# Output projections and MLP starts of a two-layer kernel: weight panels rounded one step earlier in the program, and the sum of squares behind the first MLP panel

## The reference

```
x = x + (o * silu(r)) @ w_out                       # output projection, 1024 x 1024
x = x + square(relu(rms_norm(x, g) @ w1)) @ w2      # MLP, 1024 -> 4096 -> 1024
```

## Time and profile before

| | us |
|---|---|
| median of three runs | 1702.68 |
| the profiled execution, its own time | 1700.87 |
| its span, first to last instruction | 1698.8 |
| TensorE busy | 1627.7 (96%) |
| VectorE busy | 975.7 (57%) |
| ScalarE busy | 686.7 (40%) |
| GpSimd busy | 242.0 (14%) |

### The profile page before, as it was taken

How to read it: one execution, slowest core, us unless ns; L and a number is a source line. 1 busy time by engine, 2 the same in 40 slices (tenths; PEclk the granted TensorE clock), 3 DMA queues, 4 the chain that set the end, 5 groups by cost and what they waited for, 6 DMA issues and landing times.

```text
span 1698.8 us, 24770 instructions
## 1 busy us (share of the span) xinstructions
PE 1627.7 (96%) x9418; PEld 1304.7 (77%) x9418; DVE 975.7 (57%) x1500; ACT 686.7 (40%) x1040; POOL 242.0 (14%) x222
## 2 busy tenths in 40 slices
PE   6999978999999999999799999999999999999998
PEld 3777757888888887667457888878787788888887
DVE  5555645444444457787466768586774544444443
ACT  6455543323232355424455445362543432323232
POOL 0234330000000033143200403104040000000000
PEclk7999989999999999999899999999999999999999
DMA  4222213333333334223103122131220333333333
GB/s 132 74 72 65 63 38 87 87 99 99 99 92 101 92 98 119 63 66 86 37 4 108 40 75 75 51 87 51 65 62 26 88 104 93 99 95 102 87 100 99
DMA packets 258158, 135.07 MB, mean 80 GB/s; under 512 B 10699, under 2 KB 254940, under 8 KB 258068
## 3 DMA queue, kind: packets, MB, share of 16 engines
q1 hardware_dynamic: 258068, 133.84, 28.1%
HBM read 131.64 MB, written 2.18 MB: 79 GB/s over the span
## 4 chain that ended last, share of the span: by engine, by line
PE 78%; DVE 9%; issue 7%; ACT 4%; POOL 1%; DMA 0%; DVEq 0%; POOLq 0%; PEldq 0%; ACTq 0%; SPq 0%; PEld 0%
PE bank L231 18%; PE bank L233 18%; PE bank L232 18%; PE bank L1680 4%; PE bank L493 3%; PE bank L495 3%; PE bank L494 3%; DVE arena L1985 2%; DVE w_lo L215 2%; ACT w_hi L211 1%; PE bank L1260 1%; PE bank L1514 1%; PE bank L1696 1%; PE bank L1733 1%; DVE arena L2127 1%
## 5 line engine op out<-in xcount | busy, mean ns | idle before, releaser
L211 ACT CAST w_hi<-raw 128x1024 fp32r<-128x1024 f32 x234 | 245.0, 1047 | 260.4 <-PE bank L233 237.3
L231 PE MATMUL bank<-m_hi,w_hi 128*128 128x512 f32 x856 | 337.5, 394 | 6.0 <-POOL w_lo L221 2.8
L233 PE MATMUL bank<-m_hi,w_lo 128*128 128x512 f32 x856 | 334.3, 391 | 0.0
L232 PE MATMUL bank<-m_lo,w_hi 128*128 128x512 f32 x856 | 334.3, 391 | 0.0
L215 DVE TENSOR_TENSOR w_lo<-raw,w_hi 128x1024 fp32r<-128x1024 f32 x218 | 271.2, 1244 | 102.4 <-ACT w_hi L211 100.6
L231 PE MATMUL bank<-h_hi,w_hi 128*128 128x512 f32 x640 | 256.2, 400 | 10.6 <-DVE w_lo L215 6.2
L232 PE MATMUL bank<-h_lo,w_hi 128*128 128x512 f32 x640 | 252.7, 395 | 0.0
L233 PE MATMUL bank<-h_hi,w_lo 128*128 128x512 f32 x640 | 252.4, 394 | 0.0
L231 PEld LDWEIGHTS bank<-m_hi,w_hi 128*128 128x128 f32 x856 | 161.5, 189 | 43.1 <-issue 5.5
L232 PEld LDWEIGHTS bank<-m_lo,w_hi 128*128 128x128 f32 x856 | 161.5, 189 | 34.4 <-issue 1.2
L233 PEld LDWEIGHTS bank<-m_hi,w_lo 128*128 128x128 f32 x856 | 161.4, 189 | 33.9
(11 more groups left out here) (282 smaller groups left out, 2264.4 us busy)
## 6 DMA issues: line engine op xcount, KB each, us to landing
raw<-in_l_w_ff SPq DMA_DIRECT2D x64, 512.0 KB, 4.0
raw<-in_w_in SPq DMA_DIRECT2D x64, 512.0 KB, 3.8
raw<-in_w_mlp_up SPq DMA_DIRECT2D x32, 512.0 KB, 4.0
raw<-in_w_mlp_down SPq DMA_DIRECT2D x32, 512.0 KB, 4.0
raw<-in_l_w_in SPq DMA_DIRECT2D x24, 512.0 KB, 3.8
raw<-in_l_w_out SPq DMA_DIRECT2D x8, 512.0 KB, 3.7
arena<-gb_rows SPq DMA_DIRECT2D x16, 256.0 KB, 4.7
raw<-in_w_out SPq DMA_DIRECT2D x8, 512.0 KB, 4.1
```

What stands on the lines that cost most here:

```text
L211: act.copy(w_hi[q.par][:], raw[q.par][:]).then_inc(s["w_hi_ready"], 1)
L231: pe.matmul(g_bank[q.par][:], w_hi[q.par][:, k], hi[:, k], start=(k == 0), stop=False)
L232: pe.matmul(g_bank[q.par][:], w_hi[q.par][:, k], lo[:, k], start=False, stop=False)
L233: last = pe.matmul(g_bank[q.par][:], w_lo[q.par][:, k], hi[:, k], start=False, stop=(k == KT - 1))
```

## The change

Four things are moved, and no arithmetic is added or removed.

- In `act_wout` and `dve_wout` the split of panel k + 2 stands in round k, where the split of panel k + 1 stood: on ScalarE ahead of the high half and the square, on VectorE right behind the add of panel k and ahead of its low half and accumulation. The splits are the same in number and order.
- The ones matmul is taken out of `pe_wout` (now `pe_mlp_sum`) and stands behind the first of the MLP's panels. Ln and Exp (now `act_mlp_root`) stand in the MLP's second step on ScalarE, behind the split that this step begins with.
- So that the first group of each MLP can hold these, it is written out on TensorE and ScalarE; the loop has two rounds instead of three there. On VectorE the loop keeps its three rounds.
- The 39 clears are spread over the rounds k = 2 to 5 of the first projection, and the increments of `hid_ready` and `down_done` follow the projection.

```diff
@@ -839,19 +839,22 @@
             with pe.Fori(0, KT // 2 - 1) as m:
                 for u in range(2):
                     pe_panel(pe, Panel(base + 2, 2, m, u), *lay_mid[i])
+
+        def pe_mlp_sum(pe, i):
             pe.wait_ge(s["w_acc"], KT * (i + 1))
             pe.matmul(b[0][:], ones[:], mlp_acc, start=True, stop=True).then_inc(s["w_ss"], 1)
 
         def act_wout(act, base, i, gain):
             for k in range(KT):
                 q = Panel(base, 0, 0, k)
-                if k:
-                    act_split(act, q.next())
+                if k < KT - 1:
+                    act_split(act, q.next().next())
                 act.wait_ge(bank_free[q.par], q.k + 2)
                 act.activation(lay_in[i][0][:, k], x[:, k], ACT.Copy, scale=gains[:, gain + k:gain + k + 1]).then_inc(s["w_hi"], 1)
                 if k >= 2:
                     act.wait_ge(s["w_acc"], KT * i + k - 1)
                 act.activation(mlp_sq[:, k % 2], x[:, k], ACT.Square).then_inc(s["w_sq"], 1)
+        def act_mlp_root(act, i):
             act.wait_ge(s["w_ss"], i + 1)
             act.activation(r_sqr, b[0][:], ACT.Ln, scale=1.0 / D, bias=eps[:]).then_inc(s["w_ln"], 1)
             act.wait_ge(s["w_ln"], i + 1)
@@ -860,10 +863,10 @@
         def dve_wout(dve, base, i, gain):
             for k in range(KT):
                 q = Panel(base, 0, 0, k)
-                if k:
-                    dve_split(dve, q.next())
                 wait_panel(dve, q)
                 dve.tensor_tensor(x[:, k], x[:, k], g_bank[q.par][:], ALU.add).then_inc(bank_free[q.par], 1)
+                if k < KT - 1:
+                    dve_split(dve, q.next().next())
                 dve.wait_ge(s["w_hi"], KT * i + k + 1)
                 dve.scalar_tensor_tensor(lay_in[i][1][:, k], x[:, k], gains[:, gain + k:gain + k + 1],
                                          lay_in[i][0][:, k].bitcast(F32), ALU.mult, ALU.subtract).then_inc(s["h_ready"], 1)
@@ -873,6 +876,9 @@
                 else:
                     dve.wait_ge(s["w_acc"], KT * i + k)
                     dve.tensor_tensor(mlp_acc, mlp_acc, mlp_sq[:, k % 2], ALU.add).then_inc(s["w_acc"], 1)
+                if i == 0 and 2 <= k <= 5:
+                    for done in (gla_sems + gate_sems)[k - 2::4]:
+                        dve.sem_clear(done)
 
         sems("rl sqr hid_hi hid_ready down_done dn x_fin f_sq f_acc f_ss f_ln f_r f_t f_x f_h f_hi y_ps y_sb")
 
@@ -886,27 +892,32 @@
 
         def pe_mlp(pe, base, i, first):
 
-            def group(g, last_mlp):
+            def group(g, last_mlp, first_group=False):
                 for u in range(8):
                     pe_panel(pe, Panel(base, 16, g, u), *lay_in[i], s["h_ready"] if u == 0 else None, first)
+                    if first_group and u == 0:
+                        pe_mlp_sum(pe, i)
                 for u in range(8):
                     pe_panel(pe, Panel(base, 16, g, 8 + u), *lay_mid[i], s["hid_ready"] if u == 0 else None,
                              KT * GROUPS * i + KT * g + 2)
                     if last_mlp and u >= 1:
                         pe_out(pe, u - 1)
 
-            with pe.Fori(0, GROUPS - 1) as g:
+            group(0, False, True)
+            with pe.Fori(1, GROUPS - 1) as g:
                 group(g, False)
             group(GROUPS - 1, i == 1)
 
         def act_mlp(act, base, i):
             n = KT * GROUPS * i
 
-            def group(g, last):
+            def group(g, last, first_group=False):
                 for u in range(16):
                     q = Panel(base, 16, g, u)
                     if not (last and i == 1 and u == 15):
                         act_split(act, q.next())
+                    if first_group and u == 1:
+                        act_mlp_root(act, i)
                     if u < 8:
                         wait_panel(act, q)
                         act.wait_ge(s["hid_ready"], n + KT * g + u + 1)
@@ -920,7 +931,8 @@
                     elif last and u >= 9:
                         act_out(act, u - 9)
 
-            with act.Fori(0, GROUPS - 1) as g:
+            group(0, False, True)
+            with act.Fori(1, GROUPS - 1) as g:
                 group(g, False)
             group(GROUPS - 1, True)
             if i == 0:
@@ -2279,11 +2291,9 @@
             dve_gates(dve)
             dve_gla(dve)
             fence(dve, 2)
-            for done in gla_sems + gate_sems:
-                dve.sem_clear(done)
+            dve_wout(dve, N_WO0, 0, G_FFN0)
             dve.sem_inc(s["hid_ready"], 2)
             dve.sem_inc(s["down_done"], 1)
-            dve_wout(dve, N_WO0, 0, G_FFN0)
             dve_mlp(dve, N_FF0, 0)
             dve.sem_inc(s["att_done"], 1)
             dve_in1(dve)
```

## The result

| | before | after |
|---|---|---|
| median of the five runs of the first comparison, us | 1700.27 | 1685.59 |
| lowest to highest, us | 1695.72 to 1703.55 | 1681.68 to 1686.08 |
| the profiled execution, own time, us | 1700.87 | 1685.93 |
| its span, us | 1698.8 | 1684.1 |

The ratio of the times is 0.9908, with a 95% interval of 0.9887 to 0.9929. In two later comparisons the same kernel had 0.9895 (0.9875 to 0.9916) and 0.9900 (0.9880 to 0.9921). Between the medians the difference was 14.7 us in the first comparison, 17.3 and 18.5 in the two later ones. The forecast was 1685, within 1678 to 1693.

A forecast was written before the change was run, and what follows sets the result against it. TensorE, busy 96% of the span, was taken as the bound, so only its holes and slow stretches could be won. Gains of 4.0 + 4.9 + 7.8 = 16.7 us took 1700.87 to 1684.2, called 1685, range 1678 to 1693.

The forecast's parts named there:

- The sum: Gains at four places, 16.7 us off 1700.87: 1684.2, called 1685 because the runs' median was 1.8 above the profiled execution.
- A: Third panel of the first projection: loses 4.2 us to hole and low clock; 4.0 gained, 0.2 us hole left.
- B: Start of the first MLP: 4.7 us lost, 3.0 hole and 1.7 low clock; all of it gained.
- D: Start of the second MLP: 3.1 us lost to a 2.92 us hole, no slow matmul behind; all gained.
- C: Third panel of the second projection: 6.2 us lost; 4.9 gained, a 1.3 us hole left without low clock.
- the sign named for A: First matmul of panel 2 within 0.3 us of the end of panel 1, no slow matmul after it.
- The clears: 39 semaphore clears before the first projection's add: VectorE is free for A only because they go; spreading them costs nothing.
- The second MLP panel: Panel after the moved ones matmul: subtraction done by 294.9 us, wanted at 296.9, so not late.
- rival 1: Low clock comes anyway, so only holes are won: 10.4 us, 1690.5; chance 0.13.
- rival 2: Only the MLP starts gain, another wait holding the panels' rounding: 7.8 us, 1693; chance 0.09 together with rival 4.
- rival 4: No change as measured: parts of rival 1 and rival 2, 6 to 8 us gain, 1693 to 1695; 0.09 with rival 2.
- rival 3: Slower: the MLPs' written-out group waits for its code; at 1 us per panel 1716 us; chance 0.03.

The follow-up runs named there:

- e1: Kernel after with only the splits two panels ahead and the spread clears, ones matmul and loops as before; 1689.58 us, 0.9931 of the kernel before.
- e4: Kernel after with the 39 clears put back in front of the first projection; 1681.28 us, 0.9885 of the kernel before.
- e2: Kernel after with only the sum of squares behind the first MLP panel, splits and clears as before; 1691.33 us, 0.9943 of the kernel before.
- e3: Kernel before with each MLP's first group written out on TensorE and ScalarE, nothing moved; 1699.32 us, 0.9989 of the kernel before.
- e5: Kernel before with 6 to 13 unused matmuls in each of its four holes, nothing moved; 1694.93 us, 0.9972 of the kernel before.
- run 16: Not a label of a run: a verb and a count, in "engines that run 16 more panels of straight code"; no measured time belongs to it.
- e7: e6 with 12 unused matmuls on TensorE just ahead of the first fence; 1680.76 us, 0.9892 of the kernel before.
- e8: The kernel of e7 measured again; 1677.97 us, 0.9873 of the kernel before.
- e6: Kernel after with each projection's third panel running its 16 high-half matmuls before the 8 low-half ones; 1680.29 us, 0.9890 of the kernel before.

## Why the prediction was right

**The sum.** 16.7 us were forecast; 16.5 are measured in the stages, 14.7 in the median of the first comparison, and 18.6 between the medians over all runs (1700.8 of 50 runs, 1682.2 of 17). The mechanism is shown: in the traces the waits at A, B and D shrink or go, that at C shrinks to the size forecast, and the gain lies in the two stages. That the 1685 met the median of 1685.59 so closely is luck. It is 0.8 us above the sum, where the reason given for it was a difference of 1.8, and the 17 runs of the kernel after spread from 1679.2 to 1686.2.

**A.** 4.0 forecast, 3.8 measured by e1. The chain from the end of panel 0 over cast and subtraction came to 0.1 us where I put it. The hole of 0.2 us is not fixed: where the low clock ends earlier, panel 1 ends earlier too, and the hole is 0.75 us (252.66 to 253.64 less one turn, in the second profile). The stage is as long either way (60.90 to 61.05). But the sign named for A, a first matmul within 0.3 us of the end of panel 1, thus held in the first profile of the kernel after alone, and there the first matmul behind it was still slow.

**The clears.** The step "VectorE is free for it only because the 39 semaphore clears go from there" was wrong in its size. It named what held VectorE, and the clears did fill the time until the add. But after the reordering the add alone no longer sets when the subtraction starts; the cast ends level with it, and it hid them (e4).

**B and D.** 4.7 and 3.1 forecast. B is 4.7 in e2. D cannot be read alone from e2, whose stage 2 holds a change at C too. The ones matmul costs 0.86 us, not 0.94, which leaves the gain almost as it is, since both kernels have it. The second MLP panel was no new wait.

**C.** 4.9 forecast. The hole that stays was forecast as 1.3 and is 1.34. That it would bring no low clock held in all four profiles that have it (three of the kernel after, and e4). In e1 it held too, and the low clock came behind D. The 6.2 us that C was said to lose, 3.0 of it low clock, were those of one trace. Read in the same way, C lost 5.0 us in e2 and 4.8 in e3, which leaves 3.5 to 3.6 to be won, and D lost 4.7 instead of 3.1 in e3. C and D together are sound (9.3 us before, 9.5 in e3, 7.9 of it won); the split between them is one trace's chance.

**The rivals.** That the low clock comes anyway (rival 1) fell twice: in the traces of after, and in e5, where the holes alone were changed. Its doubt was sound in another form, though: a hole and the slow stretch behind it do not go together one to one (C and D in e1, e2 and e3), and runs differ by their clock even in the untouched stretches. At an equal mean clock of 0.986 the kernel before has 1695.4 us (2 runs) and the kernel after 1683.8 (5 runs), 11.6 us apart, which is about what the holes alone are (10.4). The rest of the 18.6 is a higher clock, some 6 us of it the slow matmuls behind the holes. That only the MLP starts gain (rival 2) fell with e1, and with it rival 4. The written-out group (rival 3) fell with e3; its text names VectorE among the engines that run 16 more panels of straight code, but VectorE kept its three rounds, and e3 wrote the group out on TensorE and ScalarE as the change does.

**Page and trace.** At the MLP's loop edges no wait is to be seen: TensorE is busy 340.00 of 340 us, and with one branch less (e3) the ratio is 0.9989, with 1 inside its interval. The Trainium skill (Runtime: NRT & Kernel Launch, Instruction fetch mechanics) says that a taken branch whose target is not in the current window forces a fetch of code, a stall. The rows show none at these edges; whether their targets lay outside the window, no run here shows.

**Open.** Why the middle stretch, the same code in all kernels, takes 978.2 us in one trace and 973.9 in another. It goes with how long the same matmuls take, and no run steered that. The three traces with all four holes in place or filled (before, e3, e5) have 977.9 to 978.2, the nine others 973.9 to 977.9, so the change may have a part in it. Whether it makes the stretch shorter on average is not settled.

## What to carry to other kernels

Ask of every engine's queue not only how long its work is but what stands in front of the one instruction that the bounding engine waits for; here moving the casts and subtractions by one step and one matmul behind a panel was worth 1%, with no work removed. Price a hole on TensorE with the slow matmuls behind it, which here were a third of the loss, but add them up over a stage, since from trace to trace they fall behind another hole. Where a hole can't be closed, matmuls without a use can keep the clock. Once a chain is shortened, look again at what is last in it before crediting a further edit.

## What the runs showed of the hardware that I had not expected

- One kernel's time spreads along with the clock: the 45 runs of the kernel before that have their clock on record go from 1695.0 to 1704.9 us, with mean granted clocks from 0.986 (1695.4) to 0.979 (1704.4).
- The same hole of 2.92 us at D was followed by no slow matmul in the profile of the kernel before, and by slow ones that cost 1.4 us in e1 and 1.6 in e3. Behind the hole at C they cost 3.0, 1.7 and 1.5 us (before, e2, e3).
- 12 unused matmuls in a wait of 4.2 us brought the 12 matmuls behind it to a pitch of 0.23 us (e7, e8); without them 9 to 12 of the 12 were slow, most at 0.43 us (e6, three traces of the kernel after).
- 6 to 13 unused matmuls in holes of 2.4 to 3.1 us left every wait as long as it was and took away the slow matmuls behind them (e5).
